# Output layers: two tiles multiplied side by side over the first weight chunks; recurrence: the second group of rows rounded before the first unit

## The chip, the cores and the metric

The kernel runs on one core of one Trainium2 chip. Its time is the device time of one execution in microseconds (us). The core has five engines that run their own instruction streams and wait for each other by semaphores: TensorE (PE in the profile, its weight loads PEld), VectorE (DVE), ScalarE (ACT), GpSimd (POOL) and SyncE (SP), which issues the DMAs.

## The reference, cut to what matters

Two token mixers in two layers, then a hybrid layer, over 2048 tokens of width 1024; all in float32.

```python
for layer in range(2):                      # layer 0: attention, layer 1: gated recurrence
    h = rmsnorm(x, pre_norm_w[layer])
    y = mixer(h)                            # ends with  o @ w_out (+ b_out)
    x = x + rmsnorm(y, post_norm_w[layer])
# recurrence: 8 heads of 128, q, f, i, z = split(h @ w_in), chunked scan over the tokens,
#             o = rmsnorm(o) * gnorm_w * silu(z);  y = o @ w_out
u = rmsnorm(x, norm_w) @ w_in               # hybrid layer: GLA heads and RWKV-7 (delta rule) heads
merged = concatenate([gla_out, rwkv_out])
x = rmsnorm(x + merged @ w_out, final_norm_w)
```

## The kernel before

The program is a row of stages: `attention`, an output layer, `recurrence`, an output layer, `delta_rule`, `gla`, an output layer. Each product of float32 matrices is made of three TensorE matmuls (`product`, L195 to L197): both operands are split into a rounded part `hi` (rounded by ScalarE's Copy) and a rest `lo` (a subtraction on VectorE or GpSimd).

**Output layers** (`finish_layer`, with the start of its work in `FinishHead`). The 2048 rows of `o` are 16 tiles of 128; `w_out` is 8 chunks of 128 rows, each loaded (`load`), rounded (`round_w`, ScalarE) and subtracted (`rest_w`, VectorE, L1211). `early` chunks (5 after attention, 6 after the recurrence, 5 after `gla`) lie in memory that the stage before frees in time; the others are loaded once that stage has settled. A tile of `o` is rounded by `round_tile` (ScalarE, into `hT_cut`) and its rest taken by `rest_tile` (VectorE, L1222, tile 0 only) or by `cut` on GpSimd (L1095, tiles 1 to 15), 128x1024 at once. The stages before call `round_w`, `rest_w`, `round_tile` and `rest_tile` a few times in their last units, at places written by hand. On TensorE, `first(t)` multiplies tile t by the 8 chunks in the order `fin.order`, in two halves of 512 columns (banks m0 and m1), 48 matmuls in all; for tile 0 `products` does it and waits for each chunk's rest. Then `rest(t)` of every engine normalizes a tile: copy or bias, square and sum (ScalarE), mean (VectorE), power (GpSimd), scale, add x, square again, scale; the result `o` of tile t is turned by TensorE (`turn_rows`, L317) and kept in `hT` (L325). In the last output layer nothing is turned. The order on each engine is that of `in_turn`:

```python
for t in range(NT):
    if t + 2 < NT:
        cut(t + 2)
    first(t)
    if t:
        rest(t - 1)
```

and TensorE's `rest(t)` begins with `pe.wait_ge(*s_v.by("o", t))`.

**Recurrence.** 32 units (head, group of 512 rows); `front(u)` makes four projections f, q, z, v on TensorE, `back(u)` the scan of the unit before, merged step by step. Unit 0 has its rows rounded by the output layer before (`RecurrenceHead`). Unit 1 is the first that uses the second group of rows: its 8 chunks are rounded on ScalarE (`round_h`) and subtracted on VectorE (`rest_h`, L1742) within `front(0)`, from step 25 on, because `turns(0)` names group 1; groups 2 and 3 are handled likewise in units 15 and 16. In `on_act` and `on_dve` the stage starts with `k.settle`, a wait for everything of the stage before, then small instructions on the bounds, then `in_turn`. `back(u)` starts with the products `diag` (L1452) and `l0` to `l2` (L1479), which read what VectorE, ScalarE and GpSimd make of the unit's q, k and b (`halves`, `level`, `differences`).

**Delta rule.** ScalarE starts with `split(0)`, rounds the first rows, settles and waits for `kept3`, VectorE's last clearing of memory; its `split(1)`, which rounds the next weights, comes in the first block after that.

Of the kernel before, what the change touches and what calls it, by code (L numbers as in the profile page):

```python
# [19 lines left out]
KC = D // P  # L20
G = 512
NG = T // G
# [307 lines left out]
def attention(k):  # L330
# [293 lines left out]
    def on_act():  # L624
# [82 lines left out]
        def end(u):  # L707
            if u in (56, 57):
                fin.round_w()
            if u == 58:  # L710
                a.wait_ge(*Qpe.by("k", NT - 1))
                a.wait_ge(*o_v.by("o", 7))
                fin.round_tile(0)

# [27 lines left out]
    def on_dve():  # L742
# [166 lines left out]
        def end(u):  # L909
            if u in (57, 58):  # L910
                fin.rest_w()
            if u == 59:
                fin.rest_tile()
# [10 lines left out]
        (c, f_pe.by("p", NG * PAIRS - 9 + 2 * c)) for c in range(2, 5)])  # L924
    fin.bank_waits = [z_v.by("u", NG * KC - 4 + i) for i in range(2)]
    k.settle(pe, a, v, pool, sp)
    on_sp()
# [7 lines left out]
def finish_layer(k, x_in, x_out, bias, post_w, next_w, last_w, h_out=None, head=None):  # L935
# [20 lines left out]
    c_a, c_v, c_p = fin.c_a, fin.c_v, k.steps("o_rest", "lo")  # L956
    cut_by = lambda t: c_p.by("lo", t - 1) if t else c_v.by("lo")
    nw_ok = k.steps("norm_weights", "set")
# [73 lines left out]
    def on_pe():  # L1032
        def first(t):
            if t == 0:
                for n in range(2):
                    banks.take(f"m{n}", t)
                done = fin.products(2 * KC - len(fin.halves))
                for n in range(2):
                    done[n - 2].then_inc(*m_pe.did(f"m{n}"))
                return  # L1040
            if t == 1:
                k.settle(pe)
            pe.wait_ge(*cut_by(t))
            for n in range(2):
                b, before = banks.take(f"m{n}", t)
                if before is not None:
                    pe.wait_ge(*taken(*before))
                for c in fin.order:
                    ins = fin.piece(t, c, n, b)
                ins.then_inc(*m_pe.did(f"m{n}"))  # L1050

        def rest(t):
            if last_w is None:
                pe.wait_ge(*s_v.by("o", t))
                for half in range(2):
                    turn_rows(k, N, banks, junk, t, half, taken)

        in_turn(nothing, first, rest, ahead=lambda t: nxt.on_pe(t, last_use))

    def on_act():  # L1060
        cut = fin.round_tile

        def rest(t):
            s0, y, x = 8 * (t % 2), y_at[t % 2], x_at[t % 2]
            if y_a is not None:
                for n in range(2):
                    a.wait_ge(*m_pe.by(f"m{n}", t))
                    if t >= 2 and n == 0:
                        a.wait_ge(*s_p.by("root1", t - 2))
                    act(a, y[:, n * 512:(n + 1) * 512], banks.at(f"m{n}", t), ACT.Copy).then_inc(*y_a.did(f"y{n}"))  # L1070
            if post_w is not None:
                a.wait_ge(*y_ok.by("y1", t))
                if t >= 1:
                    a.wait_ge(*N["pe"].by("t1", t - 1))
                act(a, junk, y, ACT.Square, accum=st[:, s0:s0 + 1]).then_inc(*s_a.did("sq0"))
            a.wait_ge(*s_v.by("new", t))
            act(a, y, x, ACT.Square, accum=st[:, s0 + 4:s0 + 5]).then_inc(*s_a.did("sq1"))

        for done in ready:
            a.wait_ge(*done)  # L1080
        if not fin.tile_rounded:
            cut(0)
        for _ in range(min(2, early - fin.rounded)):
            fin.round_w()
        cut(1)
        while fin.rounded < KC:
            if fin.rounded == early:
                k.settle(a)
            fin.round_w()
        in_turn(cut, nothing, rest, ahead=lambda t: nxt.on_act(t))  # L1090

    def on_pool():
# [14 lines left out]

        cut(1)
        k.settle(pool)
        in_turn(cut, nothing, rest, ahead=lambda t: nxt.on_pool(t))  # L1110

    def on_dve():
# [35 lines left out]

        if not fin.tile_rest:
            fin.rest_tile()  # L1150
# [24 lines left out]
class FinishHead:  # L1175


    def __init__(self, k, w_out, freed):
# [9 lines left out]
        self.loaded = self.rounded = self.rests = 0  # L1188
        self.tile_rounded = self.tile_rest = False
        self.halves, self.bank_waits = [], []  # L1190

# [22 lines left out]
    def round_tile(self, t):  # L1214
        k = self.k
        act(k.act, self.part(k.hT_cut, t), self.part(k.oT, t), ACT.Copy).then_inc(*self.c_a.did("hi"))
        self.tile_rounded = True

    def rest_tile(self):
        k, v = self.k, self.k.dve  # L1220
        v.wait_ge(*self.c_a.by("hi", 0))
        v.tensor_tensor(self.part(k.oT_cut, 0), self.part(k.oT, 0), self.part(k.hT_cut, 0),  # L1222
                        ALU.subtract).then_inc(*self.c_v.did("lo"))
        self.tile_rest = True

# [90 lines left out]
def recurrence(k):  # L1316
# [71 lines left out]
    def turns(u):  # L1388

        return unit(u + 1)[1] if u + 1 < UN and unit(u + 1)[0] == 0 else None  # L1390

# [24 lines left out]
    def on_pe():  # L1416
# [24 lines left out]
        def back(u):  # L1441
# [4 lines left out]
            b, before = kb.take("diag", u)  # L1446
            pe.wait_ge(*Fv.by("q", u))
            if before is not None:
# [110 lines left out]
    def on_act():  # L1559
# [53 lines left out]
        def back(u):  # L1613
# [22 lines left out]
            if u == UN - 2:  # L1636
# [4 lines left out]
                fin.round_tile(0)  # L1641
            if u == UN - 1:
                fin.round_w()
                fin.round_w()
# [12 lines left out]
        for i, _ in pieces:  # L1657
            if i not in early:
                split(i, 0)
        k.settle(a)  # L1660
        a.wait_ge(*set_v.by("x0"))
        act(a, l0, l0, ACT.Exp).then_inc(*set_a.did("l0"))
# [76 lines left out]
    def on_dve():  # L1739
# [38 lines left out]
        def back(u):  # L1778
# [28 lines left out]
            if u == UN - 1:  # L1807
                fin.rest_w()
            for _ in range(4):
# [17 lines left out]
            if u >= UN - 2:  # L1827
                fin.rest_w()
            v.wait_ge(*Ba.by("rs", u))
            v.tensor_tensor(e_of(u, 6), kb.at("o", u), d_of(u, 7), ALU.mult).then_inc(*Bv.did("on"))  # L1830
# [5 lines left out]

        k.settle(v)
        v.wait_ge(*t_got.by("in"))
        v.wait_ge(*sel_got.by("in"))
# [26 lines left out]
        (4, Bv.by("dk", UN - 1)), (6, Bpe.by("o", UN - 1))])  # L1866
    fin.bank_waits = [Fa.by("thf", UN - 1), Fv.by("q", UN - 1)]
    place_states()
    on_sp()
# [7 lines left out]
def gla(k):  # L1877
# [251 lines left out]
    def on_act():  # L2129
# [82 lines left out]
        def gates(u):  # L2212
# [19 lines left out]
            if u == UN - 1:  # L2232
                a.wait_ge(*Fpe.by("z1", u))
                a.wait_ge(*Bv.by("out1", 1))
                fin.round_tile(0)
            gated(1)

# [74 lines left out]
    def on_dve():  # L2312
# [116 lines left out]
        (2 + (BN - 4 + i) % 3, Fpe.by(kinds[i], UN - 1)) for i in (1, 2, 3)])  # L2429
    fin.bank_waits = [Fv.by("q", UN - 1), Fv.by("z0", UN - 1)]  # L2430
    on_sp()
    on_pe()
# [6 lines left out]
def delta_rule(k, h_saved):  # L2439
# [360 lines left out]
    def on_act():  # L2800
# [38 lines left out]
        def front(i):  # L2839
# [29 lines left out]
            if i % 2 == 0:  # L2869
                if p == 0:  # L2870
                    yield from block("w", g, None)
                    shifted("w", fb.at("w", g), 12, 12, g_a, "", Fv.by("v", u - 1) if u else None, g_pe.by("w", g))
                    a.wait_ge(*g_v.by("w", g))
                    k.tanh(wa[0:64, :], wa[0:64, :]).then_inc(*g_a.did("tanh"))
# [70 lines left out]
        k.settle(a)  # L2945
        a.wait_ge(*set_v.by("kept3"))
        in_turn(nothing, solve, scores, carry, front)
# [293 lines left out]
```

## Time and profile before

| | |
|---|---|
| three runs | 3549.3, 3550.38, 3551.66 us (median 3550.38) |
| the profiled execution | 3549.64 us, of which the span is 3548.4 us |
| granted TensorE clock over the span | 0.986 |
| TensorE busy | 3423.6 us (96%) |
| VectorE, ScalarE, GpSimd busy | 59%, 49%, 39% |
| output layers begin at about | 674, 1862 and 3356 us |
| recurrence begins at about | 880 us, delta rule at 2065 us |

A row of a timeline has the start in us, the duration in us, the engine, the line of the kernel, the operation, what it writes and reads, how many instructions the row merges, and in brackets how long the engine had been idle before it and on whom it waited. Where rows are merged the duration is that from the first to the last.

### The profile page before, as it was taken

The numbers are of one execution on the slowest core, as the hardware profiler recorded it, in microseconds if no ns is written. First come the engines' busy times: TensorE is split into PE (matmuls) and PEld (weight loads), VectorE is DVE, ScalarE is ACT, GpSimd is POOL, SyncE is SP. The second block draws the span as 40 slices with busy tenths as digits, with TensorE's granted clock in tenths as the row PEclk, the third lists the DMA queues.
The fourth block names the chain that finished last, engine by engine and source line by source line (L and its number), as shares of the span: only waits on it lengthen the run. The fifth ranks groups of instructions, "written<-read, shape, count | busy, mean of one in ns | idle before, by whom it ended". The sixth has DMA issues, their size and how long they took to land.

```text
span 3548.4 us, 89303 instructions
## 1 busy us (share of the span) xinstructions
PE 3423.6 (96%) x37856; PEld 2765.1 (78%) x37856; DVE 2086.9 (59%) x4664; ACT 1730.0 (49%) x3161; POOL 1373.1 (39%) x1681
## 2 busy tenths in 40 slices
PE   8999998999999999999999989999999996999999
PEld 7888786688788887888877867777777775888787
DVE  4566766755666667666674446667666665343422
ACT  3455555522565656565554344544445342444432
POOL 5433331132565556556543233323232321444332
PEclk9999999999999999999999999999999997999999
DMA  4322221232111101111113331111111113222322
GB/s 138 96 66 84 60 57 48 81 101 94 34 43 31 43 26 43 31 43 31 38 44 129 137 110 39 44 44 38 44 44 44 38 32 132 72 72 72 107 94 85
DMA packets 252267, 231.66 MB, mean 65 GB/s; under 512 B 9120, under 2 KB 223072, under 8 KB 251872
## 3 DMA queue, kind: packets, MB, share of 16 engines
q1 hardware_dynamic: 251872, 225.94, 21.0%
q8 instruction: 303, 4.96, 0.6%
q14 instruction: 92, 0.75, 0.1%
HBM read 192.35 MB, written 33.55 MB: 64 GB/s over the span
## 4 chain that ended last, share of the span: by engine, by line
PE 86%; DVE 9%; ACT 3%; issue 2%; DMA 1%; POOL 1%; DVEq 0%; SPq 0%; ACTq 0%; POOLq 0%
PE bank L195 21%; PE bank L197 20%; PE bank L196 19%; PE bank L1479 2%; PE bank L593 2%; PE bank L2673 2%; PE bank L2684 1%; PE bank L618 1%; PE bank L605 1%; PE bank L2687 1%; DVE oT L3108 1%; PE bank L2707 1%; PE bank L2742 1%; PE bank L2699 1%; PE bank L317 1%
## 5 line engine op out<-in xcount | busy, mean ns | idle before, releaser
L196 PE MATMUL bank<-hT_cut,arena_cut 128*128 128x512 f32 x2048 | 805.5, 393 | 0.0
L189 ACT ACTIVATE arena<-bank 128x512 f32<-128x512 f32 (+1 forms) x584 | 316.2, 570 | 491.7 <-PE bank L197 299.1
L195 PE MATMUL bank<-hT_cut,arena_cut 128*128 128x512 f32 x1240 | 551.2, 445 | 2.2 <-DVE hT_cut L1742 2.0
L197 PE MATMUL bank<-hT_cut,arena_cut 128*128 128x512 f32 x1240 | 488.2, 394 | 0.0
L195 PE MATMUL bank<-arena_cut,hT_cut 128*128 128x512 f32 (+1 forms) x1280 | 458.1, 358 | 16.5 <-DVE arena_cut L1211 11.1
L189 ACT ACTIVATE arena<-arena 128x512 f32<-128x512 f32 (+3 forms) x674 | 358.5, 557 | 195.0 <-POOL arena L1681 148.3
L196 PEld LDWEIGHTS bank<-hT_cut,arena_cut 128*128 128x128 f32 x2048 | 387.6, 189 | 77.9 <-issue 17.8
L196 PE MATMUL bank<-arena_cut,hT_cut 128*128 128x512 f32 (+1 forms) x1280 | 447.0, 349 | 0.0
L190 ACT ACTIVATE arena<-arena 128x256 f32<-128x256 f32 (+2 forms) x336 | 210.3, 627 | 412.7 <-DVE arena L179 192.6
L2954 POOL TENSOR_TENSOR arena_cut<-arena,arena_cut 128x256 fp32r<-128x256 f32 x272 | 218.8, 834 | 401.9 <-ACT arena_cut L189 401.9
L727 POOL TENSOR_TENSOR arena_cut<-arena,arena_cut 128x256 fp32r<-128x256 f32 x288 | 217.9, 784 | 392.8 <-ACT arena_cut L189 392.6
L195 PE MATMUL bank<-oT_cut,arena_cut 128*128 128x512 f32 x808 | 347.7, 430 | 6.2 <-POOL arena_cut L2954 4.1
L189 ACT ACTIVATE arena_cut<-arena 128x1024 fp32r<-128x1024 f32 (+2 forms) x338 | 295.4, 888 | 73.9 <-DMA arena<-in_attn_w_in 36.2
L197 PE MATMUL bank<-oT_cut,arena_cut 128*128 128x512 f32 x808 | 318.5, 394 | 0.0
L197 PE MATMUL bank<-arena_cut,oT_cut 128*128 128x512 f32 x768 | 304.8, 397 | 0.0
L1672 POOL TENSOR_TENSOR arena_cut<-arena,arena_cut 128x256 fp32r<-128x256 f32 x248 | 209.7, 878 | 224.7 <-ACT arena_cut L189 224.7
L195 PEld LDWEIGHTS bank<-hT_cut,arena_cut 128*128 128x128 f32 x1240 | 233.6, 188 | 77.3 <-issue 25.7
L195 PEld LDWEIGHTS bank<-arena_cut,hT_cut 128*128 128x128 f32 x1280 | 241.4, 189 | 64.8 <-DVE arena_cut L1211 13.3
L197 PEld LDWEIGHTS bank<-hT_cut,arena_cut 128*128 128x128 f32 x1240 | 233.2, 188 | 53.4
L196 PEld LDWEIGHTS bank<-arena_cut,hT_cut 128*128 128x128 f32 x1280 | 241.6, 189 | 34.7 <-issue 1.7
L197 PE MATMUL bank<-arena_cut,hT_cut 128*128 128x256 f32 x896 | 250.6, 280 | 0.0
L189 ACT ACTIVATE arena<-bank,arena 128x512 f32<-128x512 f32 (+1 forms) x176 | 89.9, 559 | 283.0 <-PE bank L197 252.3
(267 smaller groups left out, 7147.0 us busy)
## 6 DMA issues: line engine op xcount, KB each, us to landing
arena<-in_w_in SPq DMA_DIRECT2D x100, 512.0 KB, 3.9
arena<-in_attn_w_in SPq DMA_DIRECT2D x144, 256.0 KB, 2.8
arena<-in_rec_w_in SPq DMA_DIRECT2D x62, 512.0 KB, 4.1
x_after<-arena SPq DMA_DIRECT2D x32, 512.0 KB, 2.6
arena<-x_after SPq DMA_DIRECT2D x32, 512.0 KB, 4.1
arena<-in_x SPq DMA_DIRECT2D x16, 512.0 KB, 3.5
h_after<-hT SPq DMA_DIRECT2D x4, 2048.0 KB, 7.7
hT<-h_after SPq DMA_DIRECT2D x4, 2048.0 KB, 16.5
```

Source lines behind the costliest of these rows:

```text
L189: return e.activation(out, a, f, bias=bias, scale=scale)
L190: return e.activation(out, a, f, bias=bias, scale=scale, accum_out=accum)
L195: pe.matmul(out, a[0], b[0], start=start, stop=False)
L196: pe.matmul(out, a[0], b[1], start=False, stop=False)
L197: return pe.matmul(out, a[1], b[0], start=False, stop=stop)
L317: ins = pe.transpose(b[:, j * P:(j + 1) * P], h[:, c * P:(c + 1) * P], k.c("ident"))
L593: ins = pe.matmul(pair[par][:, j * 256 + lo:(j + 1) * 256], qT[rows, blk * P:(blk + 1) * P], k_pair[t % 2][rows, g, lo // P:2, :], start=T ...
L727: ins = pool.tensor_tensor(w_lo[n % WN][:, c, :], raw[n % WN][:, c, :], w_hi[n % WN][:, c, :], ALU.subtract)
L1479: ins = pe.matmul(b[first:first + S, t0 // 2:(t0 + W) // 2], e[:, t0:t0 + S], view(e[:, t0:t0 + W], H)[:, :, 1, :], start=True, stop=True)
L1672: ins = pool.tensor_tensor(w_lo[i][:, c, :], raw[i][:, c, :], w_hi[i][:, c, :], ALU.subtract)
L2673: ins = mm(b4[half(1 - c), h, j, :], m5(s)[half(c), h, 0, j, 0, :], xz5(s)[half(c), 0, h, j, :], start=True, stop=True)
L2954: ins = pool.tensor_tensor(w_lo[n % 3][:, c:c + 2, :], raw[n % 3][:, c:c + 2, :], w_hi[n % 3][:, c:c + 2, :], ALU.subtract)
```

## The change

In the output layers tile 1 gets its rounding and rest ahead, as tile 0 has it: `round_tile` is called for tile 1 in the last units of the stage before (or at the start of the output layer), and its rest is made by VectorE (`rest_tile`) and no longer by GpSimd's `cut(1)`. TensorE multiplies tile 0 by the early chunks, then tile 1 by the early chunks, then tile 0 by the late chunks, then tile 1 by the late chunks; `first(1)` does nothing any more. In the recurrence ScalarE and VectorE round group 1 directly after `settle`, before the instructions on the bounds. The products `diag` wait for k in place of q. In the delta rule ScalarE's wait for `kept3` comes later, ahead of the first instruction that needs it.

```diff
@@ -710,7 +710,8 @@
                 a.wait_ge(*o_v.by("o", 7))
-                fin.round_tile(0)
+            if u in (58, 59):
+                fin.round_tile(u - 58)
@@ -909,7 +910,7 @@
                 fin.rest_w()
-            if u == 59:
+            if u in (59, 60):
                 fin.rest_tile()
@@ -923,6 +924,7 @@
     fin.bank_waits = [z_v.by("u", NG * KC - 4 + i) for i in range(2)]
+    fin.bank_waits_1 = [z_v.by("u", NG * KC - 2 + i) for i in range(2)]
     k.settle(pe, a, v, pool, sp)
@@ -954,7 +956,7 @@
     c_a, c_v, c_p = fin.c_a, fin.c_v, k.steps("o_rest", "lo")
-    cut_by = lambda t: c_p.by("lo", t - 1) if t else c_v.by("lo")
+    cut_by = lambda t: c_p.by("lo", t - 2) if t >= 2 else c_v.by("lo", t)
     nw_ok = k.steps("norm_weights", "set")
@@ -1032,14 +1034,26 @@
             if t == 0:
-                for n in range(2):
-                    banks.take(f"m{n}", t)
-                done = fin.products(2 * KC - len(fin.halves))
+                pair = [banks.take(f"m{n}", i)[0] for i in range(2) for n in range(2)][2:]
+                fin.products(2 * early - len(fin.halves))
+                for done in fin.bank_waits_1:
+                    pe.wait_ge(*done)
+                pe.wait_ge(*cut_by(1))
+                for c in fin.order[:early]:
+                    for n in range(2):
+                        fin.piece(1, c, n, pair[n])
+                done = fin.products(2 * (KC - early))
                 for n in range(2):
                     done[n - 2].then_inc(*m_pe.did(f"m{n}"))
+                for c in fin.order[early:]:
+                    for n in range(2):
+                        ins = fin.piece(1, c, n, pair[n])
+                        if c == fin.order[-1]:
+                            ins.then_inc(*m_pe.did(f"m{n}"))
+                k.settle(pe)
                 return
             if t == 1:
-                k.settle(pe)
+                return
             pe.wait_ge(*cut_by(t))
@@ -1078,11 +1092,8 @@
             a.wait_ge(*done)
-        if not fin.tile_rounded:
-            cut(0)
-        for _ in range(min(2, early - fin.rounded)):
-            fin.round_w()
-        cut(1)
+        for t in range(fin.tiles_rounded, 2):
+            cut(t)
         while fin.rounded < KC:
@@ -1105,7 +1116,6 @@
-        cut(1)
         k.settle(pool)
@@ -1146,7 +1156,7 @@
-        if not fin.tile_rest:
+        while fin.tiles_rest < 2:
             fin.rest_tile()
@@ -1186,8 +1196,8 @@
         self.loaded = self.rounded = self.rests = 0
-        self.tile_rounded = self.tile_rest = False
-        self.halves, self.bank_waits = [], []
+        self.tiles_rounded = self.tiles_rest = 0
+        self.halves, self.bank_waits, self.bank_waits_1 = [], [], []
@@ -1214,14 +1224,15 @@
         act(k.act, self.part(k.hT_cut, t), self.part(k.oT, t), ACT.Copy).then_inc(*self.c_a.did("hi"))
-        self.tile_rounded = True
+        self.tiles_rounded += 1
...
         k, v = self.k, self.k.dve
-        v.wait_ge(*self.c_a.by("hi", 0))
-        v.tensor_tensor(self.part(k.oT_cut, 0), self.part(k.oT, 0), self.part(k.hT_cut, 0),
+        t = self.tiles_rest
+        v.wait_ge(*self.c_a.by("hi", t))
+        v.tensor_tensor(self.part(k.oT_cut, t), self.part(k.oT, t), self.part(k.hT_cut, t),
                         ALU.subtract).then_inc(*self.c_v.did("lo"))
-        self.tile_rest = True
+        self.tiles_rest += 1
@@ -1387,7 +1398,7 @@
-        return unit(u + 1)[1] if u + 1 < UN and unit(u + 1)[0] == 0 else None
+        return unit(u + 1)[1] if 0 < u < UN - 1 and unit(u + 1)[0] == 0 else None
@@ -1444,7 +1455,7 @@
             b, before = kb.take("diag", u)
-            pe.wait_ge(*Fv.by("q", u))
+            pe.wait_ge(*Fv.by("k", u))
             if before is not None:
@@ -1640,6 +1651,7 @@
             if u == UN - 1:
+                fin.round_tile(1)
                 fin.round_w()
@@ -1658,6 +1670,8 @@
         k.settle(a)
+        for c in range(KC):
+            round_h(1, c)
         a.wait_ge(*set_v.by("x0"))
@@ -1805,7 +1819,7 @@
             if u == UN - 1:
-                fin.rest_w()
+                fin.rest_tile()
             for _ in range(4):
@@ -1826,6 +1840,8 @@
                 fin.rest_w()
+            if u == UN - 1:
+                fin.rest_w()
             v.wait_ge(*Ba.by("rs", u))
@@ -1835,6 +1851,8 @@
         k.settle(v)
+        for c in range(KC):
+            rest_h(1, c)
         v.wait_ge(*t_got.by("in"))
@@ -1865,6 +1883,7 @@
     fin.bank_waits = [Fa.by("thf", UN - 1), Fv.by("q", UN - 1)]
+    fin.bank_waits_1 = [Fv.by("z", UN - 1), Fa.by("v", UN - 1)]
     place_states()
@@ -2233,6 +2252,7 @@
                 fin.round_tile(0)
+                fin.round_tile(1)
             gated(1)
@@ -2428,6 +2448,7 @@
     fin.bank_waits = [Fv.by("q", UN - 1), Fv.by("z0", UN - 1)]
+    fin.bank_waits_1 = [Fv.by("z1", UN - 1), Ba.by("ln0", UN - 1)]
     on_sp()
@@ -2869,6 +2890,8 @@
                     yield from block("w", g, None)
+                    if u == 0:
+                        a.wait_ge(*set_v.by("kept3"))
                     shifted("w", fb.at("w", g), 12, 12, g_a, "", Fv.by("v", u - 1) if u else None, g_pe.by("w", g))
@@ -2943,7 +2966,6 @@
         k.settle(a)
-        a.wait_ge(*set_v.by("kept3"))
         in_turn(nothing, solve, scores, carry, front)
```

## Rows read from the trace of the kernel before

**Rows 1.** The waits of TensorE over the whole span: us, times, longest us.

```profile
PE bank L195 <- DVE arena_cut L1211: 11.1, 5, 2.8
PE bank L195 <- DVE hT_cut L1742: 9.3, 4, 6.9
```

**Rows 2.** Timeline of TensorE where the first output layer begins.

```profile
678.89 0.50 PE L195 MATMUL bank<-arena_cut,hT_cut 128*128 128x512 f32 x1 [2.27 <-DVE arena_cut L1211]
...
698.59 1.03 PE L317 MATMUL bank<-common_table,arena 128*128 128x128 f32 x8
```

**Rows 3.** Instructions of line L1211, whole span: count, ns min/median/max, starts.

```profile
L1211 DVE TENSOR_TENSOR arena_cut<-arena,arena_cut x24: 1210/1216/3408, 642.9 to 3368.7; 128x1024 fp32r<-128x1024 f32 x24
```

**Rows 4.** The same, of 675 to 676 us.

```profile
L1211 DVE TENSOR_TENSOR arena_cut<-arena,arena_cut x1: 3265/3265/3265, 675.6 to 675.6; 128x1024 fp32r<-128x1024 f32 x1
```

**Rows 5.** Timeline of GpSimd in that stretch.

```profile
675.38 2.38 POOL L1095 TENSOR_TENSOR oT_cut<-oT,hT_cut 128x1024 fp32r<-128x1024 f32 x1 [30.03 <-ACT hT_cut L189]
```

**Rows 6.** Timeline of VectorE in the first output layer, tile 0's chain.

```profile
687.00 1.29 DVE L1125 TENSOR_TENSOR arena<-bank,arena 128x512 f32<-128x512 f32 x2 [0.19 <-PE bank L197]
...
694.89 0.75 DVE L179 TENSOR_SCALAR arena<-arena 128x1024 f32<-128x1024 f32 x1 [0.66 <-POOL arena L1100]
```

**Rows 7.** Timeline of TensorE where the second output layer begins.

```profile
1867.51 0.50 PE L195 MATMUL bank<-arena_cut,hT_cut 128*128 128x512 f32 x1 [1.94 <-DVE arena_cut L1211]
...
1871.97 0.50 PE L195 MATMUL bank<-arena_cut,hT_cut 128*128 128x512 f32 x1 [2.79 <-DVE arena_cut L1211]
...
1876.41 0.39 PE L195 MATMUL bank<-arena_cut,hT_cut 128*128 128x512 f32 x1
...
1887.60 1.03 PE L317 MATMUL bank<-common_table,arena 128*128 128x128 f32 x8
```

**Rows 8.** Timeline of VectorE there, the end of tile 0's chain.

```profile
1883.92 0.75 DVE L179 TENSOR_SCALAR arena<-arena 128x1024 f32<-128x1024 f32 x1 [0.66 <-POOL arena L1100]
```

**Rows 9.** Timeline of TensorE where the third output layer begins.

```profile
3362.07 0.50 PE L195 MATMUL bank<-arena_cut,hT_cut 128*128 128x512 f32 x1 [2.69 <-DVE arena_cut L1211]
...
3366.54 0.50 PE L195 MATMUL bank<-arena_cut,hT_cut 128*128 128x512 f32 x1 [1.39 <-DVE arena_cut L1211]
```

**Rows 10.** Timeline of VectorE there.

```profile
3360.80 9.08 DVE L1211 TENSOR_TENSOR arena_cut<-arena,arena_cut 128x1024 fp32r<-128x1024 f32 x6
```

**Rows 11.** Timeline of TensorE where the recurrence begins.

```profile
899.77 0.77 PE L195 MATMUL bank<-oT_cut 128*128 128x512 f32 x1 [6.88 <-DVE hT_cut L1742]
...
908.70 0.50 PE L195 MATMUL bank<-oT_cut 128*128 128x512 f32 x1
```

**Rows 12.** Timeline of VectorE there.

```profile
880.78 1.29 DVE L325 TENSOR_TENSOR hT<-bank,arena 128x512 f32<-128x512 f32 x2 [1.95 <-PE bank L317]
888.61 1.09 DVE L1840 CAST arena<-oT 128x1792 int8<-128x1792 f32 x1 [6.54 <-DMA oT<-select]
```

**Rows 13.** Timeline of ScalarE there.

```profile
897.93 4.25 ACT L189 ACTIVATE oT_cut<-hT 128x512 fp32r<-128x512 f32 x8
```

**Rows 14.** Timeline of GpSimd there.

```profile
899.03 1.18 POOL L1681 TENSOR_TENSOR arena<-arena 128x256 f32<-128x256 f32 x1
```

**Rows 15.** Timeline of TensorE where the delta rule begins.

```profile
2065.13 1.97 PE L317 MATMUL bank<-common_table,arena 128*128 128x128 f32 x8 [7.47 <-DVE arena L179]
...
2077.76 0.50 PE L195 MATMUL bank<-oT_cut,arena_cut 128*128 128x512 f32 x1 [0.93 <-POOL arena_cut L2954]
```

**Rows 16.** Timeline of ScalarE there.

```profile
2073.67 1.06 ACT L189 ACTIVATE arena_cut<-arena 128x1024 fp32r<-128x1024 f32 x1 [5.08 <-DVE arena L3181]
```

**Rows 17.** Stretches of 2 us: us, busy by engine, granted clock, DMA share, GB/s.

```profile
3360.00:3362.00 2.00, 0.00 (x0) 0.00 (x0) 1.97 (x4) 2.00 (x4) 0.00 (x0) 1.00 0.00 0
897.00:899.00 2.00, 0.00 (x0) 0.00 (x0) 0.42 (x1) 1.60 (x4) 2.00 (x4) 0.50 0.00 0
1874.00:1876.00 2.00, 2.00 (x6) 1.52 (x6) 1.31 (x1) 0.30 (x1) 2.00 (x2) 0.50 0.28 113
2072.00:2074.00 2.00, 2.00 (x6) 1.52 (x6) 1.44 (x12) 0.33 (x1) 0.00 (x0) 0.51 1.03 342
```

## The prediction, made before the changed kernel ran

> **What bounds the kernel now.** I read part 1 of the page first: TensorE is busy 96% of the span, so only its idle time, its clock and the order of its work can move the end. The view of TensorE's waits came next. Its largest entries are the ones that this change is aimed at: the rests of `w_out` chunks (11.1 us in five waits) and the rests of the recurrence's rows (9.3 us in four, one of 6.9) [rows 1]. The timelines of each engine at the three output layers and at the start of the recurrence and of the delta rule then show where each wait lies and what the other engines do meanwhile, and the windows give the granted clock around them [rows 17]. In all, the change can reach some 20 us of idle time, 0.6% of the kernel. It can also create new idle time, because it changes the order on the engine that is the bound.
>
> Spacing of matmuls: 84 of them run from 678.89 to 698.59, 0.2345 us each [rows 2]; 48 from 1876.41 to 1887.60, 0.233 each [rows 7].
>
> **First output layer.** TensorE waits 2.27 us for the rest of the third chunk [rows 2]. That subtraction took 3.265 us [rows 4], where the median is 1.216 [rows 3]; GpSimd's `cut(1)` ran beside it from 675.38 for 2.38 us [rows 5]. The change takes `cut(1)` away from there, so the rest should end at 675.6 + 1.2 = 676.8, and TensorE goes on at about 676.85: 2.0 us gained. From there to the end of tile 1 are 84 matmuls, 19.7 us, to 696.55. But the new order ends tile 0 only 18 matmuls (three late chunks) before that, at 696.55 − 4.2 = 692.3. Before, tile 0 ended 36 matmuls after 678.89, at 687.3, and its result was there at 694.89 + 0.75 = 695.64 [rows 6], 8.3 us later. With the same 8.3 us it is now there at 700.6. TensorE's next step after both tiles is `rest(0)`, the transposes of tile 0, which wait for that result, since `first(1)` is now empty and `first(2)` stands behind `rest(0)`. They started at 698.59 and will start at 700.7: **+2.1 us**, with TensorE idle for 4.1. What is queued behind this wait on TensorE is all of tiles 2 to 15. The loss is not made up, because the loop behind it is bound by TensorE.
>
> **Second output layer.** Chunk six is used from 1867.51, and chunk seven, which comes late by DMA, from 1871.97 after a wait of 2.79 us [rows 7]. The 12 matmuls after that ran at half clock (granted 0.50 [rows 17]): 4.44 us in place of 2.80. Now tile 1's first six chunks, 36 matmuls, fill that wait: from 1867.51 run 6 + 36 + 12 matmuls of both tiles until tile 0 ends, 54 × 0.233 = 12.6, so 1880.1, and 12 more to 1882.9. Tile 0 ended at 1876.41 and its result came at 1883.92 + 0.75 = 1884.67 [rows 8], 8.26 later. Now it comes at 1888.35, and the transposes start at 1888.5 and not at 1887.60: **+0.9 us**. 4.7 us of TensorE's time were saved and are waited away again, with 5.5 us of idle time.
>
> **Third output layer.** Nothing is turned here, so nothing waits for tile 0. ScalarE's rounding of tile 1 (1.06 us for this shape [rows 16]) is put ahead of the work that produces the last gate, and VectorE's rest of tile 1 (1.2 [rows 3]) ahead of the third chunk's rest, which starts at 3360.80 without idle time before it [rows 10]. It starts 2.2 later, at 3363.0, and ends at 3364.2; TensorE, which went on at 3362.07 [rows 9], idles 5 us and goes on at 3364.25. From there 84 matmuls take 19.6, to 3383.9. Before, it stopped once more, until 3366.54 [rows 9], and 72 matmuls led to 3383.3: **+0.6 us**. The wait of 1.39 goes since tile 1's work covers it; the longer first wait takes its place.
>
> **Tails of attention and recurrence.** Each gets one rounding of 1.06 us and one subtraction of 1.2. I cost them at nothing: they fall in the time in which ScalarE and VectorE wait for the last units' products. If that cover is gone, they cost up to 2.3 us in each of the two tails; that belongs to the range. The new waits for banks (`bank_waits_1`) and for tile 1's rest come after tile 0's early chunks and name work that is then done, so they cost nothing.
>
> **Start of the recurrence.** TensorE stops for 6.88 us until 899.77 [rows 11], since ScalarE rounds group 1 only at 897.93, in eight steps of together 4.25 us [rows 13], behind the decay chain. The clock then is 0.50 [rows 17]. With the change the rounds run right after settling, when VectorE's last write ends at 880.78 + 1.29 = 882.07 [rows 12]: to 886.4 on ScalarE, with the rests just behind on VectorE, which otherwise waits until 888.61 (6.54 us) for a table [rows 12]. So TensorE goes on at 892.9 with 24 matmuls of f, to 898.5. What is late next is the unit's own decay chain: GpSimd's last difference of the second level ends at 899.03 + 1.18 = 900.2 [rows 14], then an exp and a product follow, about half a us each (an estimate from 4.25/8 per step [rows 13]), and the last level's matmuls, so q of unit 1 starts near 901.9 and not at 908.70 [rows 11]: 6.8. I take 0.3 off because VectorE's rests may reach a little past 888.61: **−6.5 us**. Bounds: −9.2 if that chain does not bind (898.5 and a us for the products between), −2 if the rests push VectorE's small instructions and with them the whole chain.
>
> `diag` waiting for k in place of q: in the trace these products never wait for q, so it costs nothing and saves nothing.
>
> **Start of the delta rule.** ScalarE's rounding of the next weights waits 5.08 us for a clearing by VectorE [rows 16], GpSimd's rest follows, and TensorE waits 0.93 for it [rows 15]. The wait is moved behind the rounding: **−0.9 us** (bounds 0 and −0.9).
>
> **Clock.** The sum so far is 2.1 + 0.9 + 0.6 − 6.5 − 0.9 = −3.8. New gaps of 4.1, 5.5 and 5 us come in. The trace shows the clock at half after gaps of 6.88, 2.79 and 7.47 us, and at full in the gap of 2.69 [rows 7, 9, 11, 15, 17]. So a new gap costs either nothing, or about what the one of 2.79 did: 4.44 − 2.80 = 1.64 [rows 7]. The upper bound is the delta rule's: half clock from 2065.13 until about 2074 [rows 15, 17], 8.9 us, of which a busy array loses half, 4.4. I take two of three gaps at 1.7: **+3.4**. Sum −0.4.
>
> The Trainium skill (page "TensorE: Matmul & The Clock Gate", section "HAM oscillation — how this bites in real kernels") warns that idle gaps between bursts of matmuls send the array back to half rate, again at each gap. By that rule all three new gaps would cost, and the sum would be −3.8 + 3 × 1.7 = +1.3 in place of −0.4; the trace's gap of 2.69 without a fall speaks for the lower count only for gaps as short as that.
>
> The profiled execution took 3549.64, 0.74 below the median of the three runs. 3549.64 − 0.4 = 3549.2, with 0.74 added **3550.0**.
>
> **Rivals.** 0.2% is 7.1 us, about what a measurement can tell from no change: faster means below 3543.3, slower above 3557.5.
> - *The new order does not stall* (0.12). If tile 0's chain took under 4.2 us in the first layer and 2.8 in the second, the transposes would start when tile 1 ends: −2.0, and 1882.9 − 1887.6 = −4.7. With +0.6 − 6.5 − 0.9 that is −13.5: 3536.9. Against it: the same chain took 8.3 and 8.26, and nothing in it becomes shorter.
> - *The clock falls in every new gap and stays down as long as at the delta rule* (0.11): −3.8 + 3 × 4.4 = +9.4, 3559.8. It decides slower from 3.6 us per gap on. For it: the gap of 2.79 was enough for a fall. Against it: that one cost 1.64.
> - *The recurrence gains little* (0.15): group 1's rests hold up the small instructions of unit 0 and the decay chain; −2 in place of −6.5, so 3554.5. For it: VectorE has only 6.54 us of room for eight rests that can start no earlier than ScalarE. That the change does nothing there is within this.
> - *The forecast* (0.62): own range 3544 to 3554 (each gap 0 to 1.7, the recurrence −9.2 to −4.5).
>
> The range 3540 to 3557 leaves out most of the first and second rival. Faster: 0.12 and 0.04 from the forecast's lower edge with no fall of the clock, 0.16. Slower: 0.11 and 0.01, 0.12. Same: 0.72.
>
> **What the changed profile would show.** Right: an entry of TensorE's waits at L317 for VectorE's L179 of about 4 us near 697 and 5.5 us near 1883; the third chunk's rest at 1.2 us near 676; no gap of 6.9 us near 893, and q of unit 1 some 6.5 us nearer to the transposes before it; a gap of about 5 us near 3359; no wait of 0.93 at the delta rule. Wrong, if TensorE shows no wait at the first transposes of a layer; if the granted clock near 1888 or 3364 is 0.50 for more than 4 us; or if VectorE's first small instructions of the recurrence come more than 1 us later against the settling than now.

## The result, and the profile after

The changed kernel takes 3552.51 us (median of 20 runs, 3547.22 to 3557.36), the kernel before 3546.46 in the same comparison (20 runs, 3542.12 to 3551.66). The ratio is 1.0014, interval 1.0008 to 1.0021: slower by 5 us, 3 to 7. The forecast was 0.4 us faster. The time lies in the range of the prediction, the sign does not agree with it. That the time fits is luck in part: the three runs that the forecast was added to have a median 3.9 us above that of the 20 runs.

The two profiled executions differ by 0.9 us only (spans 3548.4 and 3549.3). The first kernel's was one of its slower runs: 3549.64 beside a median of 3546.46. So the two traces can't be subtracted as wholes. They are compared stretch by stretch, from one instruction to another that is the same in both.

TensorE's waits in the changed kernel, over the whole span (us in total, times, longest), beside [rows 1]:

```profile
PE bank L317 <- DVE arena L179: 17.0, 3, 7.5
...
PE bank L195 <- DVE arena_cut L1221: 6.5, 3, 4.8
PE bank L1490 <- DVE arena L1786: 5.9, 6, 1.5
...
PE bank L195 <- DVE hT_cut L1756: 2.0, 2, 1.8
```

The wait for the recurrence's rows fell from 9.3 to 2.0, that for the weight chunks from 11.1 to 6.5. In their place stand the transposes (17.0; one wait of 7.5 of them was there before, [rows 15]) and the recurrence's level products, L1490 (5.9; 3.3 before, then L1479). TensorE's timeline of the changed kernel at the places that change, in order of time:

```profile
676.85 0.50 PE L195 MATMUL bank<-arena_cut,hT_cut 128*128 128x512 f32 x1 [0.22 <-DVE arena_cut L1221]
...
700.75 1.10 PE L317 MATMUL bank<-common_table,arena 128*128 128x128 f32 x8 [4.04 <-DVE arena L179]
...
714.40 1.04 PE L317 MATMUL bank<-common_table,arena 128*128 128x128 f32 x8
...
883.81 1.03 PE L317 MATMUL bank<-common_table,arena 128*128 128x128 f32 x8
...
903.40 0.45 PE L1490 MATMUL bank<-arena 128*32 128x16 f32 x32 [1.01 <-DVE arena L1786]
905.03 0.45 PE L1490 MATMUL bank<-arena 128*32 128x16 f32 x32 [1.18 <-DVE arena L1786]
906.59 0.63 PE L1490 MATMUL bank<-arena 128*32 128x16 f32 x32 [1.11 <-DVE arena L1786]
907.14 0.80 PE L195 MATMUL bank<-oT_cut 128*128 128x512 f32 x1
...
967.28 0.46 PE L1463 MATMUL bank<-arena 128*32 128x32 f32 x32
...
1867.07 0.50 PE L195 MATMUL bank<-arena_cut,hT_cut 128*128 128x512 f32 x1 [1.56 <-DVE arena_cut L1221]
1888.18 1.94 PE L317 MATMUL bank<-common_table,arena 128*128 128x128 f32 x8 [5.45 <-DVE arena L179]
...
1902.46 1.03 PE L317 MATMUL bank<-common_table,arena 128*128 128x128 f32 x8
...
3354.59 0.47 PE L195 MATMUL bank<-arena_cut,hT_cut 128*128 128x512 f32 x1 [0.84 <-DVE oT_cut L1233]
3362.40 0.80 PE L195 MATMUL bank<-arena_cut,hT_cut 128*128 128x512 f32 x1 [4.77 <-DVE arena_cut L1221]
...
3540.95 0.39 PE L197 MATMUL bank<-arena_cut,oT_cut 128*128 128x512 f32 x1
```

Two things are to be seen. The three new gaps are where the forecast put them and nearly as long: 4.04, 5.45 and 4.77 us. And after each of them, as after the three short waits of 903 to 907, TensorE runs at half clock for a while. The windows show it (us, busy by engine, granted clock, DMA; a granted clock of 1.00 is full speed, 0.50 half); in layer 2 the clock falls while TensorE still stands in the wait:

```profile
702.00:704.00 2.00, 2.00 (x6) 1.53 (x5) 1.90 (x4) 0.07 (x1) 0.82 (x1) 0.50 0.61 229
1886.00:1888.00 2.00, 0.00 (x0) 0.00 (x0) 0.88 (x2) 2.00 (x5) 1.10 (x2) 0.52 0.64 262
1888.00:1890.00 2.00, 1.82 (x9) 1.85 (x10) 0.72 (x2) 0.34 (x1) 2.00 (x1) 0.50 0.49 160
1890.00:1892.00 2.00, 2.00 (x6) 1.57 (x6) 0.85 (x2) 1.15 (x2) 0.61 (x2) 0.50 0.27 107
1892.00:1894.00 2.00, 2.00 (x8) 1.58 (x7) 1.75 (x2) 0.00 (x0) 0.18 (x1) 0.78 0.00 0
3362.00:3364.00 2.00, 1.60 (x4) 1.33 (x5) 2.00 (x3) 0.00 (x0) 0.00 (x0) 0.50 0.95 385
908.00:910.00 2.00, 2.00 (x6) 1.52 (x6) 2.00 (x5) 0.63 (x1) 1.30 (x3) 0.54 0.00 0
```

The account by stretches, from five instructions of the trace before that answer to these (the second transposes of layer 1 began at 710.67, the last ones of that layer at 880.15 and unit 3's `diag` at 967.65, the second transposes of layer 2 at 1899.67, the last product at 3540.01):

| stretch | before | after | difference |
|---|---|---|---|
| layer 1: start of the third chunk's wait to the second transposes | 34.05 | 37.77 | +3.7 |
| recurrence: layer 1's last transposes to unit 3's `diag` | 87.50 | 83.47 | −4.0 |
| layer 2: start of the sixth chunk's wait to the second transposes | 34.10 | 36.95 | +2.85 |
| delta rule: layer 2's last transposes to the delta rule's first products of line L2707 (now L2728) | 45.35 | 43.07 | −2.3 |
| layer 3: first to last product | 183.66 | 186.36 | +2.7 |

The sum is +3.0, at the lower edge of what the runs measured.

### The profile page after: what moved, and what is told of

Read it like the earlier page. It is cut to its first block, busy times and chain, and to the rows that moved or that the text cites. A ratio compares the mean times of both kernels' runs of the same rounds, so it can differ in the third digit from the quotient of the medians.

```text
span 3549.3 us, 89306 instructions
## 1 busy us (share of the span) xinstructions
PE 3426.0 (97%) x37856; PEld 2767.0 (78%) x37856; DVE 2091.9 (59%) x4667; ACT 1730.4 (49%) x3161; POOL 1366.4 (38%) x1678
## 4 chain that ended last, share of the span: by engine, by line
PE 85%; DVE 9%; ACT 3%; issue 2%; POOL 1%; DMA 0%; DVEq 0%; ACTq 0%; SPq 0%; POOLq 0%
PE bank L195 21%; PE bank L197 19%; PE bank L196 19%; PE bank L1490 2%; PE bank L593 2%; PE bank L2694 2%; PE bank L2705 1%; PE bank L618 1%; PE bank L605 1%; PE bank L2708 1%; DVE oT L3130 1%; PE bank L2728 1%; PE bank L2763 1%; PE bank L317 1%; PE bank L2720 1%
```

## The experiments

All ratios below are to the kernel before, which ran on the same chip each time (medians 3548.46 in the first four runs, 3549.8 in the second four).

**recur_only**: the recurrence's and the delta rule's part of the diff applied to the kernel before.

```
 # kernel before, plus only: turns(), round_h/rest_h after settle, diag, kept3
-        pe.wait_ge(*Fv.by("q", u))
+        pe.wait_ge(*Fv.by("k", u))
...
         k.settle(a)
+        for c in range(KC):
+            round_h(1, c)
```

> The kernel before with the recurrence's and the delta rule's edits alone (group 1 rounded ahead, diag waits for k, the wait for kept3 moved), the output layers as before. Theory A, read from the two traces place by place: the recurrence gives 3.7 us back and not 6.5, the delta rule about 2.4, so 6 us faster than before (ratio 0.9983). Rival B: what the recurrence gains at its start is lost again in its levels, so only the delta rule's 1 to 2 us remain (ratio 0.9995 or more).

Measured 3540.64 us, ratio 0.9979 (0.9970 to 0.9988): theory A's size, and no sign of rival B. The stretch of the recurrence's start is 83.73 us (−3.8), that of the delta rule 42.42 (−2.9).

**out_only**: the changed kernel with exactly those lines taken back.

> The changed kernel with the recurrence's and the delta rule's edits undone, so the output layers' edits alone. Theory A: each of the three layers loses about 3 us, two in transposes that wait for tile 0, and in all three by the clock, so 9 us slower than before (ratio 1.0026). Rival B: the loss is 3.6 us as in the sum of the forecast without the clock (ratio 1.0010), and the rest of the loss is the recurrence's.

Measured 3559.13 us, ratio 1.0026 (1.0017 to 1.0035), as theory A has it; rival B's 1.0010 is outside the interval. So the output layers' edits alone cost 9 us. The rest of the change gives about 4 back by the difference of this run and the changed kernel, 7 by `recur_only`; the intervals allow both. What is lost lies in the output layers, not in the recurrence; which of their edits loses it, the next run tells.

**old_order**: the changed kernel, TensorE's order alone as before.

```
-                for c in fin.order[:early]:
-                    for n in range(2):
-                        fin.piece(1, c, n, pair[n])
                 done = fin.products(2 * (KC - early))
...
-                for c in fin.order[early:]:
+                for c in fin.order:
```

> The changed kernel with TensorE's old order: tile 0 by all chunks, then tile 1 by all; the rounding and rest of tile 1 stay ahead on ScalarE and VectorE. Theory A: the waits of the first transposes go in layers 1 and 2; layer 1 gains 2.0 against before since GpSimd no longer slows the third chunk's rest, layer 2 is as before with its wait of 2.8 and its half clock, layer 3 still loses by the late third chunk (about 1 to 3), the recurrence and delta rule gain 6: 5 to 7 us faster than before (ratio 0.9981 to 0.9986). Rival: if the interleaving is not what costs, the time is that of the changed kernel (ratio 1.0014).

Measured 3544.05 us, ratio 0.9990 (0.9981 to 0.9999): faster than before and clearly apart from the changed kernel. The middle of the interval is less gain than theory A said, though the interval reaches theory A's 0.9981 to 0.9986. The transposes of layers 1 and 2 wait no more, so it is TensorE's order that made them wait; layer 3 still takes 2.7 more than before (186.38), since the late third chunk stays (a wait of 4.78), which TensorE's order does not change. Layer 2 is 1.6 shorter than before (32.47), which theory A did not expect: its wait is 3.15, but the clock stays at 1.00 behind it. Layer 1 takes 33.02 us from the wait to the second transposes, 1.0 less than before and not 2.0. The missing part is a wait for the sixth chunk, which now comes into reach (the second row):

```profile
675.82 0.50 PE L195 MATMUL bank<-arena_cut,hT_cut 128*128 128x512 f32 x1 [0.21 <-DVE arena_cut L1225]
681.06 0.50 PE L195 MATMUL bank<-arena_cut,hT_cut 128*128 128x512 f32 x1 [0.77 <-DVE arena_cut L1225]
696.56 1.04 PE L317 MATMUL bank<-common_table,arena 128*128 128x128 f32 x8
```

**best1**: as old_order, with two chunks of tile 1 ahead in layer 2 and tile 1's work later in layer 3.

```
+                fin.products(2 * early - len(fin.halves))
+                if fin.ahead:                      # 0, 2, 0 in the three layers
+                    second(fin.order[:fin.ahead])
+                done = fin.products(2 * (KC - early))
...
+                second(fin.order[fin.ahead:])
```

> As the one before, but in layer 2 the first two chunks of tile 1 go between tile 0's early and late chunks, as much as fills the wait of 2.8 us; in layer 3 tile 1 is rounded after the early chunks and its rest taken after all chunks. Theory A: layer 1 -2.0, layer 2 -4.5 (no wait and no half clock, transposes start when tile 1 ends), layer 3 -1.4, recurrence and delta rule -6: 14 us faster than before (ratio 0.9961). Rival: tile 0's result still comes after tile 1's end in layer 2, or the third layer's first wait grows: 8 to 10 us (ratio 0.9975).

Measured 3540.83 us, ratio 0.9980 (0.9972 to 0.9989): the rival's 0.9975 lies in the interval, theory A's 0.9961 does not. Layer 2 does what it should (the transposes wait 0.26, layer 2 is shorter by 4.0), but layer 3 is not better than before: the rest of tile 1, put behind all chunks, ran beside GpSimd's `cut` of later tiles and took 3.43 us in place of 1.2, and TensorE waited 0.82 for it. First VectorE's row, then GpSimd's:

```profile
3360.93 3.43 DVE L1241 TENSOR_TENSOR oT_cut<-oT,hT_cut 128x1024 fp32r<-128x1024 f32 x1
```

```profile
3360.88 5.74 POOL L1112 TENSOR_TENSOR oT_cut<-oT,hT_cut 128x1024 fp32r<-128x1024 f32 x2 [30.14 <-ACT hT_cut L189]
```

**filled**: the changed kernel with useless products in the two waits for tile 0's result. They are not part of the computation and their bank is overwritten later.

```
                 k.settle(pe)
+                for c in range(fin.fill):          # 5, 7, 0 in the three layers
+                    product(pe, k.bank[6], (part(k.hT_cut, 1)[:, c, :], part(k.oT_cut, 1)[:, c, :]),
+                            (fin.wo_hi[:, c, 0:512], fin.wo_lo[:, c, 0:512]), start=True, stop=True)
                 return
```

> The changed kernel, with useless products written to a free bank while TensorE waits for tile 0's result: 15 matmuls (3.5 us) in the first layer's wait of 4.0, 21 (4.9) in the second's of 5.45. Nothing else changes, and the wait still ends with tile 0's result. Theory A: the clock, which fell after these waits, stays at full; 1.6 us less lost in layer 1 and 2.0 in layer 2, so 3 to 4 us under the changed kernel (ratio to before about 1.0004). Rival: the loss behind the waits is something else (queues, the chain of tile 1), and the time is the changed kernel's (1.0014).

Measured 3549.01 us, ratio 1.0004 (0.9995 to 1.0013), theory A's number. The interval overlaps that of the changed kernel (1.0008 to 1.0021), so the times alone do not settle it; the stretches do: layer 1 is 1.6 us shorter than in the changed kernel (36.16), layer 2 2.25 (34.70), layer 3 the same (186.39). More work on TensorE made these layers faster. The transposes still start when tile 0's result is there, 0.45 us after the last useless product, and the clock stays at full:

```profile
1888.04 1.10 PE L317 MATMUL bank<-common_table,arena 128*128 128x128 f32 x8 [0.45 <-DVE arena L179]
1900.17 1.03 PE L317 MATMUL bank<-common_table,arena 128*128 128x128 f32 x8
...
1890.00:1892.00 2.00, 2.00 (x10) 1.60 (x9) 0.95 (x3) 0.38 (x2) 0.77 (x2) 1.00 0.36 137
```

Ten matmuls in two us, where the changed kernel had six. From one transposes to the next are 12.13 us here and 14.28 there.

**rec_late**: recur_only, with unit 0's `diag` and levels some six chunks later on TensorE.

```
-            for _ in range(6):
+            for _ in range(6 if u else 11):
                 yield
             b, before = kb.take("diag", u)
```

> The kernel before with the recurrence's and the delta rule's edits, and unit 0's diag and levels put some six chunks of q later on TensorE. Theory A: the recurrence's edit gains only 3.8 us at its start and not 6.5 because the three level products wait 3.3 us for VectorE's chain in turn and the clock then falls for 1.3; with q's products ahead of them, both go: 3 to 4 us faster than recur_only (ratio to before 0.9970). Rival: the chain of unit 0 is late anyway and the waits come back at its later steps: the same as recur_only (0.998).

Measured 3539.55 us, ratio 0.9973 (0.9963 to 0.9984). The interval overlaps recur_only's, so the times alone do not tell the theories apart. The trace does: of the three waits one of 0.23 is left, the granted clock stays at 1.00 from 898 to 906, and the stretch to unit 3's `diag` is 81.05 us, 6.45 less than before. That the whole time gains so little over `recur_only` has a place too: the delta rule's stretch is 45.64 us here and 42.42 there, where the clock did not fall in it.

```profile
900.27 0.46 PE L1452 MATMUL bank<-arena 128*32 128x32 f32 x32
900.54 0.77 PE L1479 MATMUL bank<-arena 128*32 128x16 f32 x64
901.54 0.45 PE L1479 MATMUL bank<-arena 128*32 128x16 f32 x32 [0.23 <-DVE arena L1774]
```

**layers2**: the kernel before with mended output layers alone: one chunk of tile 1 ahead in layer 1, two in layer 2, none in layer 3, where tile 1's rest stands between the early and the late chunks' rests.

> The kernel before with output layers of the mended kind alone: tile 1 goes ahead by one chunk in layer 1, two in layer 2, none in layer 3, where its rest lies between the early and the late chunks' rests. Theory A: layer 1 -1.5 to -2.0, layer 2 -3, layer 3 -1.4: 6 us faster than before (ratio 0.9983). Rival: as seen in the mended kernel so far the layers bring about 1 us in sum (0.9997).

Measured 3541.24 us, ratio 0.9978 (0.9969 to 0.9987). Theory A's 0.9983 lies in the interval, the rival's 0.9997 does not. By stretches layer 1 is 2.1 us shorter than before (31.99) and layer 2 3.9 (30.19); layer 3 takes 183.53, as before, so the 1.4 that theory A expected there did not come. The delta rule's stretch is 1.7 shorter (43.68) without any edit in it.

**best2**: both together, the output layers of `layers2` with the recurrence's and the delta rule's edits as in `rec_late`.

> The two before together: mended output layers, the recurrence's and the delta rule's edits, late levels in unit 0. Theory A: the sum of both, 14 to 17 us faster than before (ratio 0.9955). Rival: 8 us as recur_only alone (0.9978).

Measured 3535.02 us (5 runs), ratio 0.9963 (0.9950 to 0.9975): faster than both kernels. Theory A's 0.9955 lies in the interval, the rival's 0.9978 just outside. Layer 1 is 2.1 us shorter than before, the recurrence's start 6.5, layer 2 2.9, the delta rule 2.95; layer 3 is the same as before (183.53 us). In layer 3 the second chunk wait is gone, but the clock now fell after the gap of 2.69, which it had not in the trace before [rows 9, 17]:

```profile
3344.19 0.50 PE L195 MATMUL bank<-arena_cut,hT_cut 128*128 128x512 f32 x1 [2.69 <-DVE arena_cut L1230]
...
3346.00:3348.00 2.00, 2.00 (x6) 1.52 (x5) 1.54 (x2) 1.06 (x1) 0.00 (x0) 0.50 0.96 358
```

**small**: the kernel before with `diag`'s and `kept3`'s edits alone.

> The kernel before with the two small edits alone: diag waits for k, and the wait for kept3 comes later. A look at the trace. Theory A: nothing moves until the delta rule; there TensorE gains 1.0 by the second block of products and 2.3 by 60 us after its start, as in the four traces that have the edit. Rival: only the 0.9 us of the one wait that was named is gained, and what is more in the other traces came from the shifted start.

One execution of each was timed, 3542.60 us and 3547.78 for the kernel before; that tells nothing of the change, so only stretches are read. At the recurrence nothing moves by more than 0.3 us. The delta rule's stretch takes 42.98 us, 2.4 less than before. By the third block of products 0.7 of it is gained, by the waits; the other 1.6 is the clock, which in the kernel before falls after the third block's wait (0.66 in the first window, of the kernel before) and here does not (1.00 in the second, of this run):

```profile
2100.00:2104.00 4.00, 3.94 (x10) 2.53 (x11) 3.41 (x5) 1.19 (x1) 4.00 (x4) 0.66 0.34 103
```

```profile
2098.00:2102.00 4.00, 4.00 (x18) 2.94 (x17) 3.04 (x4) 0.23 (x1) 4.00 (x5) 1.00 0.07 20
```

**before_again**: the kernel before, unchanged.

> The kernel before once more, unchanged: a second trace. Theory A: the 1.4 to 2.8 us by which the traces differ in attention, and the 3 us by which the changed kernel's differs in the last part of the delta rule, are changes from run to run with the clock at half or full in the same stretches, so this trace differs from the first by as much without any edit. Rival: both belong to the edits, and this trace agrees with the first within 0.5 us up to 2900 us.

One execution, 3545.77 us: the span is 3544.5 us, 3.9 less than in the first trace of the same kernel. It stands 2.7 us ahead of it already at layer 1, 2.6 at the start of the delta rule and 4.1 at its end (2997.56 and 2993.43). At both places the clock differs. First the windows of the first trace: it runs partly at half between 20 and 40 us, in attention between 610 and 620, and in the delta rule between 2970 and 2990:

```profile
20.00:40.00 20.00, 17.83 (x127) 17.43 (x126) 9.10 (x17) 9.81 (x18) 12.58 (x19) 0.77 0.29 79
...
610.00:620.00 10.00, 7.66 (x37) 6.52 (x36) 7.47 (x26) 7.06 (x19) 1.90 (x3) 0.83 0.10 29
...
2970.00:2990.00 20.00, 16.03 (x364) 13.02 (x366) 9.94 (x31) 3.84 (x10) 0.00 (x0) 0.74 0.01 3
```

The same windows of the second trace:

```profile
20.00:40.00 20.00, 17.22 (x138) 17.09 (x137) 9.84 (x17) 10.44 (x19) 13.18 (x20) 0.91 0.30 82
...
610.00:620.00 10.00, 7.67 (x47) 6.04 (x45) 6.83 (x19) 6.95 (x19) 3.23 (x4) 1.00 0.10 28
...
2970.00:2990.00 20.00, 13.64 (x446) 11.19 (x446) 11.94 (x38) 4.97 (x13) 0.00 (x0) 0.99 0.01 3
```

So differences of 1.6 to 2.7 us come from run to run without any edit, and the one of 3 us between the traces of the two kernels in the last part of the delta rule need not be the change's. The rival is refuted. One more thing differs between these two traces of one kernel: after the same gap of 2.69 us in layer 3 the clock stayed at full in the first [rows 9, 17] and fell in the second:

```profile
3358.00:3360.00 2.00, 1.76 (x4) 1.47 (x5) 2.00 (x3) 1.18 (x2) 1.69 (x1) 0.52 0.89 272
```

## Why the prediction was wrong

**Layer 1** was right. The third chunk's rest was free of GpSimd, TensorE went on 2.05 us earlier, tile 0's result was late, and the transposes started 2.15 us later than before against the same instruction (forecast +2.1), after a wait of 4.04 (forecast 4.1).

**Layer 2** was right: from the sixth chunk's product to the transposes 21.11 us against 20.09, +1.0 (forecast +0.9), wait 5.45 (forecast 5.5).

**Layer 3** was right in its mechanism. The third chunk is used 7.81 us after the first and not 5.72, 2.1 later (forecast 2.2). With 84 products of 0.233 behind it, and before 72 behind the second wait (10.19 after the first), that is 27.4 against 27.0, +0.4 (forecast +0.6).

**The clock** was mis-sized. The step that failed is "I take two of three gaps at 1.7", +3.4. All three fell, and two cost more: from one transposes to the next 13.65 us against 12.08 in layer 1, so 1.6; 14.28 against 12.07 in layer 2, 2.2; and in layer 3 2.7 less the 0.4 above, 2.3. That is +6.1. The price of 1.64 came from a gap of 2.79, after which the clock fell only when TensorE had been at work again for some 0.6 us. In the waits of 5.45 and 4.77 it had fallen before the work went on (0.50 from 1886.5 and from 3361.0), and it stayed at 0.50 for some 4.7 us of work from 1888.18 and 5.0 from 3362.40. The forecast had named this as a sign of being wrong, 0.50 for more than 4 us near 1888 or 3364. `filled` shows that it is the clock and nothing else behind the first two waits: with the array kept busy, both extra times go. For layer 3 no run shows it apart; there it is the rest of a sum. The Trainium skill (page "TensorE: Matmul & The Clock Gate", section "HAM oscillation — how this bites in real kernels") had the stronger statement, that each such gap costs, and the trace agrees: granted 0.50 after each of the three. The one gap that spoke for a lower count, 2.69 without a fall, says nothing on gaps of 4 to 5.5, as the forecast itself remarked, and `before_again` shows that the same gap can fall too.

**The start of the recurrence** is the other failed term: −6.5 forecast, −4.0 measured (5.22 us earlier at unit 1's q, 23.33 us after the transposes against 28.55, and 1.2 lost again in the six half-clock products behind it). The step that failed is what follows on GpSimd's last difference: "then an exp and a product follow, about half a us each". From the end of that difference to q the forecast has 1.7 us (900.2 to 901.9), the trace 3.2 (903.94 to 907.14). Each level has two such products on VectorE (L1785 and L1786) and not one; they were priced with the half us of a rounding; and the two engines were taken to work freely beside each other. In the changed kernel VectorE's six products of the first three levels and GpSimd's differences run at the same time, and each product takes 0.72 to 0.95:

```profile
901.87 0.72 DVE L1785 TENSOR_TENSOR arena<-arena 128x256 f32<-128x256 f32 x1 [1.14 <-ACT arena L189]
902.52 0.83 DVE L1786 TENSOR_TENSOR arena<-arena 128x256 f32<-128x256 f32 x1
903.27 0.95 DVE L1785 TENSOR_TENSOR arena<-arena 128x256 f32<-128x256 f32 x1
904.14 0.83 DVE L1786 TENSOR_TENSOR arena<-arena 128x256 f32<-128x256 f32 x1
904.89 0.88 DVE L1785 TENSOR_TENSOR arena<-arena 128x256 f32<-128x256 f32 x1
905.70 0.83 DVE L1786 TENSOR_TENSOR arena<-arena 128x256 f32<-128x256 f32 x1
```

```profile
903.03 0.91 POOL L1695 TENSOR_TENSOR arena<-arena 128x256 f32<-128x256 f32 x1
...
904.65 0.84 POOL L1695 TENSOR_TENSOR arena<-arena 128x256 f32<-128x256 f32 x1
```

Instructions of the same lines take 0.41 on VectorE at 908.40, where GpSimd is idle, and 0.61 on GpSimd at 901.13, where VectorE is idle:

```profile
908.40 0.41 DVE L1786 TENSOR_TENSOR arena<-arena 128x256 f32<-128x256 f32 x1
```

```profile
901.13 0.61 POOL L1694 TENSOR_TENSOR arena<-arena 128x256 f32<-128x256 f32 x1
```

The Trainium skill (page "SBUF — State Buffer", section "🔬 SBUF: two separate sides") has the rule: a VectorE instruction with two inputs from that memory and a GpSimd instruction hold one pair of ports in turn. The trace agrees with it: 0.83 for 0.41. The forecast reckoned with such a slowing, from rows, for the chunk's rest in layer 1 and not for the chain that it made the new bound. It also saw one late product, where three stand one behind the other and each waits 1.0 to 1.2 us for its own step of the chain. No run parts the number of products from their slowing. `rec_late` shows that these waits and the clock behind them are all that was missing: with q's products ahead of them the gain is 6.45.

**The delta rule** gave −2.3 and not −0.9. The waits gave 0.7 by the third block (forecast 0.9); 1.6 more is a fall of the clock after that block which the trace before has and this one does not, and which the forecast did not count. That the edit takes it away is not shown: of the eight traces with the edit six are without the fall, but `rec_late` and `best1` have it, and `layers2`, which does not have the edit, is without it too. `diag` waiting for k moved nothing (`small`), as forecast.

The sum with what was measured: 2.15 + 1.0 + 0.4 + 6.1 − 4.0 − 2.3 = +3.4, inside the 3 to 7 of the runs (the table's +3.0 also counts that the sixth chunk's wait was 0.4 shorter). With clock and recurrence as forecast it is −1.9, so these two terms decide the sign. Of the rivals, "The recurrence gains little" (−2 in place of −6.5) and "The clock falls in every new gap" (4.4 each) each came about half true. The recurrence gained 4.0, and not the rests held it up: they ended at 892.6, and VectorE's scan of the decay began 14.15 us after the writing of the last rows began, before it was 14.02. The clock did fall in every gap, at 1.6 to 2.3 each.

What is left open: why the clock falls behind one and the same gap in one execution and not in another. No run here tells that, and the length of the gap alone does not: in layer 2 the gap of 2.79 was followed by 0.50 [rows 7, 17], longer ones at the same place, of 3.15 in `old_order` and 3.21 in `recur_only`, by 1.00, and in `recur_only` layer 2 was 1.5 us shorter without an edit in it:

```profile
1868.47 0.50 PE L195 MATMUL bank<-arena_cut,hT_cut 128*128 128x512 f32 x1 [3.21 <-DVE arena_cut L1211]
...
1869.00:1871.00 2.00, 2.00 (x10) 1.60 (x9) 2.00 (x2) 1.24 (x3) 1.66 (x1) 1.00 0.98 401
```

## What to carry to other kernels

Work that fills a wait must be no longer than the wait. Six chunks of tile 1 in front of a chunk that came 2.8 us late moved tile 0's end by more than the wait, and tile 0's result was the next thing needed; two chunks filled the same wait and won 3 to 4 us. When a wait is taken away, price the chain that is next with the durations that its instructions have when they run beside each other, not alone, and count each step of it that TensorE meets in order. An idle gap on TensorE costs its length and, where the clock falls, the half clock behind it, 1.6 to 2.3 us in the three gaps here; if it can't be removed, useless products in it gave the second part back in the two layers where this was tried.

## What the runs showed of the hardware that was not expected

A gap of 2.69 us at the same place of one kernel left the clock at full in one trace [rows 17] and was followed by 0.52 in the next (`before_again`), and a gap of 3.21 us left it at full (`recur_only`): the price of a gap of this length is not fixed. Three waits of 1.0 to 1.2 us with a few small products between them were followed by 0.54, though none is long by itself. And one and the same kernel differs by 3.9 us in the spans of two traces, which drift apart where the granted clock is lower in one of them (0.74 against 0.99 in the delta rule); a change of 5 us is seen only in many runs or stretch by stretch.
